# Conv-state transposes between half sums, a second gate product in spare PSUM banks, and the last tile's squares summed in PSUM

## The chip, the cores and the metric

The kernel runs on one core of a Trainium2 chip. The metric is the device time in microseconds of one execution; the median of a few timed runs counts.

## The reference

One layer of a decoder trunk for 512 prompt tokens and 8 sample tokens, in float32. The change touches its last part, cut here to what matters:

```
a, g = split(rmsnorm(h) @ w_up)                  # 1024 -> 2 x 2816
ac = conv_b + causal conv of width 3 over a      # the last rows of a are the new conv state
h = h + (gelu(ac) * g) @ w_down                  # 2816 -> 1024
gate = sigmoid(rmsnorm(h) @ w_ple_gate)          # 1024 -> 1024
h = h + gate * (p @ w_ple)                       # 256 -> 1024
y = rmsnorm(h)                                   # final norm, with the gain g_final
```

Outputs are y for both groups, the recurrent states, and the conv state: 2 rows of 2816 for the prompt, and for each of the 8 samples its old second row and one new row.

## The kernel before

The kernel keeps all activations transposed: channels on partitions, the 520 tokens along the free dimension, split into two halves of 260 that fill the two banks of a PSUM accumulator. Each float32 operand is split into a high and a low part (`whi`/`wlo` for weights, `xah`/`xal`, `xbh`/`xbl`, `ach`/`acl`, `pxh`/`pxl` for activations), and a product is three matmuls (high x high, high x low, low x high) per chunk of 128 rows and token half, six per chunk. `product` (L459) issues them on TensorE (PE). Weights come in units; SP loads `raw`, ScalarE (ACT) copies it to `whi`, VectorE (DVE) subtracts to get `wlo`. Two units are in flight, and ACT and DVE prepare the unit two ahead (`ahead`) when PE has finished one.

Sections run in a fixed order: A, V, B, C, D, E, then F (up-projection and conv, 11 rounds of 4 units), G (down-projection), and H (gates and per-layer input). Each engine follows its own program in order, joined by counting semaphores. There is no planner: the order is written out.

**G.** Each of 8 output tiles of 128 channels needs 22 chunks, in two half sums of 11 chunks (66 matmuls each), so 16 half sums in 4 rounds of 4. After the second half sum of a tile, DVE adds it to `hT` (`residual`), ACT writes `xbh`, DVE writes `xbl`, and GpSimd (POOL) adds the tile's squares to `ssq`.

**H.** For each output tile `j` PE computes a gate product of 8 chunks (48 matmuls) into `acc[0]` and a linear product of 2 chunks (12 matmuls) into `acc[1]`, then `y_tile(j-1)`: one transpose of the sample columns into `ob` and four transposes of 128 tokens into a bank of `lvb`. Within the first gate product PE computes the mean squares (`mean_square(1)`), from which ACT and DVE make `rstd`. DVE forms `tg` = gate product x `rstd` (L1473), ACT its sigmoid `sgg` (L1081), DVE `tp` = linear product x `sgg` (L1477) and `hT` += `tp` (L1479). ACT writes `yT` = `hT` x gain (L1086), `y_copy` brings the transposed tile from `lvb` to `ytok`, and POOL adds the tile's squares. The second gate product waits until `tg` of the first has been read out of `acc[0]`.

**The tail.** After the last product PE transposes the conv state `cs` (22 chunks, 10 columns each) in six groups of up to four into the two `lvb` banks by turns; DVE and ACT copy them to `csr`. Then `y_tile(7)` follows, and the sum of `ssq` over channels (L782) into `mb`: five float32 matmuls, shown as ten instructions. ACT takes the root (L1094), DVE the reciprocal `rt` (L1492), then ACT scales columns 0 to 383 of each row block of `ytok` (L1102) and DVE columns 384 to 1023 (L1500); SP issues the stores of `csr` and then of the five row blocks, the fifth being the samples.

The PSUM tensors are `acc[0]`, `acc[1]` and `lvb` (two banks each), `ob` and `mb` (one each), all eight banks.

Of the kernel before, what the change touches and what calls it, by code (L numbers as in the profile page):

```python
# [13 lines left out]
NS = 8  # L14
# [22 lines left out]
L_C, L_F, L_Y = 8, 24, 28  # L37
# [25 lines left out]
def hybrid_layer(nc, x_prompt, x_sample, state_hgrn, state_ret, state_conv, p_prompt, p_sample,  # L63
# [180 lines left out]
    with ctx:  # L244
# [81 lines left out]
        rt_ready = sem("rt_ready")  # L326
        stored = sem("stored")
# [34 lines left out]
        def _(sp):  # L362
# [56 lines left out]
            with sp.Fori(0, 2) as it:  # L419
                for k in range(4):  # L420
                    load("H", k, it, [wpg_v[:, :, it * 4 + k, :], wpl_v[:, :, it * 4 + k, :]])
            yp = y_prompt[0].rearrange("(i p) n -> p i n", p=128)

            for b in range(2):
                sp.wait_ge(lv_free[b], L_Y // 2 + 7 - b)
            sp.dma_start(conv_prompt[0, 0], csr[0:2, :]).then_inc(stored, 16)
            sp.dma_start(conv_sample[0, :, 1, :], csr[2:10, :]).then_inc(stored, 16)
# [14 lines left out]
        def _(pe):  # L442
# [16 lines left out]
            def product(sec, k, it, slot, tile, chunks, w0, xh, xl, first=True, last=True, tper=4,  # L459
                        wait_unit=True, chunk_wait=None):  # L460
# [4 lines left out]
                if first:  # L465
                    pe.wait_ge(acc_free[tile % 2], tidx(sec, tile, it, tper))
                n = len(chunks)
                for i, c in enumerate(chunks):
# [3 lines left out]
                    for q, (wt, xx) in enumerate(((whi, xh), (whi, xl), (wlo, xh))):  # L472
                        for b in range(2):
                            mm = pe.matmul(acc[tile % 2][:, b, 0:HT], wt[slot][:, w],  # L474
# [238 lines left out]
            def mean_square(n):  # L713
# [3 lines left out]
                for b in range(2):  # L717
                    pe.wait_ge(lv_free[b], L_F // 2 + n)
# [18 lines left out]
            with pe.Fori(0, 4) as it:  # L737
                for k in range(4):
                    if k < 2:
                        pe.wait_ge(ac_lo, FC // (2 - k) + 1)  # L740
                    product("G", k, it, k % 2, k // 2, range(11 * (k % 2), 11 * (k % 2) + 11), 0, ach, acl,
                            first=k % 2 == 0, last=k % 2 == 1, tper=2)
# [15 lines left out]
            for j in range(DC):  # L758
                it, k = j // 4, j % 4
                if j == 0:  # L760
                    def wait_tile(c):
                        if c == 6:
                            mean_square(1)
                        pe.wait_ge(xb_lo, 8 + c + 1)
                product("H", k, it, k % 2, 2 * k, C8, 0, xbh, xbl, tper=8,
                        chunk_wait=wait_tile if j == 0 else None)
                product("H", k, it, k % 2, 2 * k + 1, range(2), 8, pxh, pxl, tper=8, wait_unit=False)
                if j:
                    y_tile(j - 1, j - 1)
            pe.wait_ge(cs_ready, FC)  # L770
            for n in range(6):
                wait_bank(7 + n)
# [948 lines left out]
```

## Time and profile before

| | us |
|---|---|
| median of 3 timed runs | 988.9 (987.56 to 989.34) |
| span of the profiled execution | 985.5 |
| PE busy | 961.0 (98%) |
| DVE busy | 526.4 (53%) |
| ACT busy | 394.5 (40%) |
| POOL busy | 237.7 (24%) |

The profile is of one execution and gives no total time of its own, only the span from its first instruction to its last event. Busy PE time is modelled and includes stretches at the lower clock. L12 is line 12 of the kernel. Matmul instructions overlap: the rows give each group's start and its extent.

### The profile page before, as it was taken

Reading aid. Unit: us, or ns where it says so; the run is one execution under the profiler, and the core shown is the slowest. Engines: PE = TensorE matmul, PEld = TensorE weight load, DVE = VectorE, ACT = ScalarE, POOL = GpSimd, SP = SyncE. Lnnn points to the kernel's source line nnn. Section 1 sums busy time; section 2 is a strip of 40 time slices with the busy share of each in tenths; the row PEclk is TensorE's granted clock in tenths of the full one; section 3 lists DMA queues with packets and bytes.
Section 4 is the critical chain, followed back from the end, with each engine's and each line's share of the span. In section 5 each row is a group of like instructions: output and inputs, shape, how many; then the busy total and the mean of one; then the engine's idle time right before and its main releaser. Section 6 shows DMA issues by size and latency. Waiting matters only on the chain.

```text
span 985.5 us, 20971 instructions
## 1 busy us (share of the span) xinstructions
PE 961.0 (98%) x7866; PEld 928.7 (94%) x7866; DVE 526.4 (53%) x620; ACT 394.5 (40%) x524; POOL 237.7 (24%) x279
## 2 busy tenths in 40 slices
PE   7999999999999999999999999999999999999995
PEld 6999998898989999999999999999999999999994
DVE  5332275664754555456657656655566543435454
ACT  5443345363533544443325444444443321222333
POOL 0006075756501111000362111111111131212331
PEclk9999999999999999999999999999999999999998
DMA  7222422212113332353332332223223333322212
GB/s 233 65 86 86 172 76 65 75 35 71 53 53 108 101 90 85 106 188 110 94 97 76 91 102 85 85 87 104 86 85 105 101 93 106 91 85 80 73 36 92
DMA packets 168052, 91.49 MB, mean 93 GB/s; under 512 B 13584, under 2 KB 166560, under 8 KB 167600
## 3 DMA queue, kind: packets, MB, share of 16 engines
q1 hardware_dynamic: 149698, 80.61, 27.4%
q10 hardware_dynamic: 18320, 10.42, 3.7%
q8 instruction: 22, 0.36, 0.2%
q14 instruction: 12, 0.10, 0.0%
HBM read 83.10 MB, written 8.00 MB: 92 GB/s over the span
## 4 chain that ended last, share of the span: by engine, by line
PE 96%; ACT 1%; DVE 1%; DMA 1%; issue 1%; SPq 0%; ACTq 0%; DVEq 0%
PE acc L474 82%; PE lvb L556 3%; PE ob L605 1%; PE ob L606 1%; PE mb L628 1%; PE lvb L671 1%; DMA xtok<-in_x_prompt 1%; PE mb L683 1%; PE lvb L515 0%; PE mb L593 0%; PE mb L665 0%; PE ob L661 0%; PE ob L660 0%; PE lvb L642 0%; PE lvb L523 0%
## 5 line engine op out<-in xcount | busy, mean ns | idle before, releaser
L803 ACT ACTIVATE whi<-raw 128x1024 fp32r<-128x1024 f32 (+2 forms) x132 | 146.5, 1111 | 356.0 <-PE acc L474 354.9
L1123 DVE TENSOR_TENSOR wlo<-raw,whi 128x1024 fp32r<-128x1024 f32 (+2 forms) x132 | 193.2, 1464 | 178.9 <-ACT whi L803 178.9
L474 PE MATMUL acc<-xah,whi 128*128 128x260 f32 x896 | 188.0, 291 | 0.0
L474 PE MATMUL acc<-xah,wlo 128*128 128x260 f32 x896 | 181.5, 284 | 0.0
L474 PE MATMUL acc<-xal,whi 128*128 128x260 f32 x896 | 180.9, 284 | 0.0
L474 PE MATMUL acc<-xbh,whi 128*128 128x260 f32 x832 | 169.1, 284 | 3.2 <-DVE tg L1473 2.4
L474 PE MATMUL acc<-xbh,wlo 128*128 128x260 f32 x832 | 168.3, 284 | 0.0
L474 PE MATMUL acc<-xbl,whi 128*128 128x260 f32 x832 | 168.1, 284 | 0.0
L474 PEld LDWEIGHTS acc<-xah,whi 128*128 128x128 f32 x896 | 139.2, 190 | 8.9 <-issue 8.2
L474 PEld LDWEIGHTS acc<-xah,wlo 128*128 128x128 f32 x896 | 139.0, 190 | 0.0
L474 PEld LDWEIGHTS acc<-xal,whi 128*128 128x128 f32 x896 | 139.0, 190 | 0.0
L474 PEld LDWEIGHTS acc<-xbh,whi 128*128 128x128 f32 x832 | 128.8, 189 | 3.7 <-issue 3.5
L474 PEld LDWEIGHTS acc<-xbh,wlo 128*128 128x128 f32 x832 | 129.0, 189 | 0.0
L474 PEld LDWEIGHTS acc<-xbl,whi 128*128 128x128 f32 x832 | 128.6, 189 | 0.0
L474 PE MATMUL acc<-ach,whi 128*128 128x260 f32 x352 | 70.9, 283 | 0.0
L474 PE MATMUL acc<-ach,wlo 128*128 128x260 f32 x352 | 70.8, 282 | 0.0
L474 PE MATMUL acc<-acl,whi 128*128 128x260 f32 x352 | 70.6, 282 | 0.0
L1617 POOL TENSOR_TENSOR sqt<-hT 128x520 f32 x24 | 37.4, 1556 | 130.9 <-DVE hT L1379 98.0
L1637 POOL TENSOR_TENSOR gg<-gg,cv 128x520 f32<-128x520 f32 x22 | 28.9, 1314 | 118.0 <-DVE gg L1440 115.2
L474 PEld LDWEIGHTS acc<-acl,whi 128*128 128x128 f32 x352 | 54.3, 188 | 0.0
L474 PEld LDWEIGHTS acc<-ach,whi 128*128 128x128 f32 x352 | 54.2, 188 | 0.0
L474 PEld LDWEIGHTS acc<-ach,wlo 128*128 128x128 f32 x352 | 54.1, 188 | 0.0
(283 smaller groups left out, 1253.7 us busy)
## 6 DMA issues: line engine op xcount, KB each, us to landing
raw<-in_w_in SPq DMA_DIRECT2D x96, 256.0 KB, 3.1
raw<-in_w_up SPq DMA_DIRECT2D x88, 256.0 KB, 3.1
raw<-in_w_down SPq DMA_DIRECT2D x16, 384.0 KB, 3.3
raw<-in_w_down SPq DMA_DIRECT2D x16, 320.0 KB, 3.8
raw<-in_w_out SPq DMA_DIRECT2D x16, 256.0 KB, 2.9
raw<-in_w_ple_gate SPq DMA_DIRECT2D x8, 512.0 KB, 3.7
x_transposed<-xstg SPq DMA_DIRECT2D x1, 2080.0 KB, 7.5
hT<-x_transposed ACTq DMA_DIRECT2D x1, 2080.0 KB, 9.3
```

The source lines that it names most:

```text
L474: mm = pe.matmul(acc[tile % 2][:, b, 0:HT], wt[slot][:, w], xx[:, c, b * HT:(b + 1) * HT], start=first and i == 0 and q == 0, stop=last an ...
L556: mm = pe.matmul(lvb[:, l % 2, c * 128:(c + 1) * 128], lk[l % 4][:, c, :], zq[l % 4][:, c].rearrange("k two t -> k (two t)"), start=True, ...
L605: pe.matmul(out, vst[:, h * 64:(h + 1) * 64], sfull[:, h, :], start=True, stop=False)
L606: mm = pe.matmul(out, head(sst, h), head(lq[3], h), start=False, stop=True)
L628: mm = pe.matmul(mb[64 * h2:64 * h2 + 64, b:b + 1], ss[64 * h2:64 * h2 + 64, b, :], qs8[64 * h2:64 * h2 + 64, b:b + 1], start=True, stop=True)
L671: pe.matmul(level(b), k8[:], vblk[:, 512 * b:512 * b + 512], start=True, stop=True).then_inc(lv_full, 1)
L683: mm = pe.matmul(mb[:, b:b + 1], rsm[:, b, :], qs8[:, b:b + 1], start=True, stop=True)
L803: act.activation(whi[k % 2][:, 0:n], raw[k % 2][:, 0:n], ACT.Copy).then_inc(hi_ready, 1)
L1123: dve.tensor_tensor(wlo[k % 2][:, 0:n], raw[k % 2][:, 0:n], whi[k % 2][:, 0:n].bitcast(fp), SUB).then_inc(lo_ready, 1)
L1617: step(pool.tensor_tensor(sqt[:], hT[:, j, :], hT[:, j, :], MUL))
L1637: pool.tensor_tensor(gg[:], gg[:], cv[:], MUL).then_inc(act_ready, 1)
```

## The change

- On PE the last of G's four rounds is written out. `conv_rows(n)` transposes up to four chunks of the conv state into bank `n % 2` of `lvb`; two such groups follow each of the first three half sums of this round. ACT copies the even groups and DVE the odd ones to `csr`, at the end of their work for that half sum. SP issues the two conv stores between the two rounds of H loads.
- In H the gate product of tile 1 goes into `lvb` and not into `acc[0]`. PE waits for `tg` of this tile before `y_tile(0)` writes `lvb`.
- POOL adds the squares of seven tiles. DVE squares the eighth into `tg`, and PE sums both over channels into the same columns of `mb` (`token_sums`), the older seven first. `y_tile(7)` comes last on PE; DVE scales its columns (896 to 1023) from `lvb`, and the sample columns 512 to 1023 from `ob`, straight from PSUM. ACT computes a root of a constant after its last sigmoid.

```diff
 M_B, M_C, M_F, M_G = 3, 27, 47, 48
-L_C, L_F, L_Y = 8, 24, 28
+L_C, L_F, L_S, L_H, L_Y = 8, 24, 26, 32, 34
 MERGES = LV + 1
...
         rt_ready = sem("rt_ready")
+        sq_last = sem("sq_last")
         stored = sem("stored")
...
                     load("G", k, it, [wdn_v[:, FC // 2 * (k % 2):FC // 2 * (k % 2 + 1), it * 2 + k // 2, :]])
-            with sp.Fori(0, 2) as it:
+            for it in range(2):
                 for k in range(4):
                     load("H", k, it, [wpg_v[:, :, it * 4 + k, :], wpl_v[:, :, it * 4 + k, :]])
+                if it == 0:
+                    for b in range(2):
+                        sp.wait_ge(lv_free[b], L_H // 2)
+                    sp.dma_start(conv_prompt[0, 0], csr[0:2, :]).then_inc(stored, 16)
+                    sp.dma_start(conv_sample[0, :, 1, :], csr[2:10, :]).then_inc(stored, 16)
             yp = y_prompt[0].rearrange("(i p) n -> p i n", p=128)
-            for b in range(2):
-                sp.wait_ge(lv_free[b], L_Y // 2 + 7 - b)
-            sp.dma_start(conv_prompt[0, 0], csr[0:2, :]).then_inc(stored, 16)
-            sp.dma_start(conv_sample[0, :, 1, :], csr[2:10, :]).then_inc(stored, 16)
             for i in range(5):
...
             def product(sec, k, it, slot, tile, chunks, w0, xh, xl, first=True, last=True, tper=4,
-                        wait_unit=True, chunk_wait=None):
+                        wait_unit=True, chunk_wait=None, into=None):
...
                     pe.wait_ge(lo_ready, unit(sec, k, it) + 3)
-                if first:
+                if first and into is None:
                     pe.wait_ge(acc_free[tile % 2], tidx(sec, tile, it, tper))
+                sums = acc[tile % 2] if into is None else into
                 n = len(chunks)
...
                         for b in range(2):
-                            mm = pe.matmul(acc[tile % 2][:, b, 0:HT], wt[slot][:, w],
+                            mm = pe.matmul(sums[:, b, 0:HT], wt[slot][:, w],
                                            xx[:, c, b * HT:(b + 1) * HT],
...
                 for b in range(2):
-                    pe.wait_ge(lv_free[b], L_F // 2 + n)
+                    pe.wait_ge(lv_free[b], (L_F, L_H)[n] // 2)
                     pe.matmul(lvb[:, b, 0:HT], ones1024[:], ssq[:, b * HT:(b + 1) * HT],
...
-            with pe.Fori(0, 4) as it:
-                for k in range(4):
-                    if k < 2:
-                        pe.wait_ge(ac_lo, FC // (2 - k) + 1)
-                    product("G", k, it, k % 2, k // 2, range(11 * (k % 2), 11 * (k % 2) + 11), 0, ach, acl,
-                            first=k % 2 == 0, last=k % 2 == 1, tper=2)
+            def half_sum(k, it):
+                if k < 2:
+                    pe.wait_ge(ac_lo, FC // (2 - k) + 1)
+                product("G", k, it, k % 2, k // 2, range(11 * (k % 2), 11 * (k % 2) + 11), 0, ach, acl,
+                        first=k % 2 == 0, last=k % 2 == 1, tper=2)
+            def conv_rows(n):
+                pe.wait_ge(lv_free[n % 2], L_S // 2 + n // 2)
+                for j in range(4 * n, min(4 * n + 4, FC)):
+                    mm = pe.transpose(lvb[0:10, n % 2, (j % 4) * 128:(j % 4 + 1) * 128], cs[:, j, :], ident)
+                mm.then_inc(lv_full, 1)
+            with pe.Fori(0, 3) as it:
+                for k in range(4):
+                    half_sum(k, it)
+            pe.wait_ge(cs_ready, FC)
+            for k in range(4):
+                half_sum(k, 3)
+                if k < 3:
+                    conv_rows(2 * k)
+                    conv_rows(2 * k + 1)
...
                         pe.wait_ge(xb_lo, 8 + c + 1)
+                if j == 1:
+                    for b in range(2):
+                        pe.wait_ge(lv_free[b], L_Y // 2)
                 product("H", k, it, k % 2, 2 * k, C8, 0, xbh, xbl, tper=8,
-                        chunk_wait=wait_tile if j == 0 else None)
+                        chunk_wait=wait_tile if j == 0 else None, into=lvb if j == 1 else None)
                 product("H", k, it, k % 2, 2 * k + 1, range(2), 8, pxh, pxl, tper=8, wait_unit=False)
+                if j == 1:
+                    pe.wait_ge(acc_free[0], tidx("H", 2, 0, 8) + 1)
                 if j:
                     y_tile(j - 1, j - 1)
-            pe.wait_ge(cs_ready, FC)
-            for n in range(6):
-                wait_bank(7 + n)
-                for j in range(4 * n, min(4 * n + 4, FC)):
-                    mm = pe.transpose(lvb[0:10, (7 + n) % 2, (j % 4) * 128:(j % 4 + 1) * 128], cs[:, j, :], ident)
-                mm.then_inc(lv_full, 1)
-            y_tile(7, 13)
-            pe.wait_ge(ssq_ready, 25)
+            def token_sums(t, last):
+                for i in (0, 4, 1, 2, 3):
+                    n = 128 if i < 4 else NS
+                    mm = pe.matmul(mb[0:n, i:i + 1], t[:, i * 128:i * 128 + n], ones1024[:, 0:1],
+                                   start=not last and i == 0, stop=last and i == 3)
+                return mm
+            pe.wait_ge(ssq_ready, 24)
             wait_misc(M_G, 0, 0, 0)
-            for i in range(5):
-                n = 128 if i < 4 else NS
-                mm = pe.matmul(mb[0:n, i:i + 1], ssq[:, i * 128:i * 128 + n], ones1024[:, 0:1],
-                               start=True, stop=True)
-            mm.then_inc(misc_full, 1)
+            token_sums(ssq, False)
+            pe.wait_ge(sq_last, 1)
+            token_sums(tg, True).then_inc(misc_full, 1)
+            y_tile(7, 7)
...
             def inverse_rms(n):
-                act.wait_ge(lv_full, L_F + 2 * n + 2)
+                act.wait_ge(lv_full, (L_F, L_H)[n] + 2)
                 for b in range(2):
...
                         residual("G", k // 2, it, 2, 24)
+                    if nxt and k < 3:
+                        w = min(512, FF - 2 * k * 512)
+                        act.wait_ge(lv_full, L_S + 2 * k + 1)
+                        act.activation(csr[:, 2 * k * 512:2 * k * 512 + w], lvb[0:10, 0, 0:w],
+                                       ACT.Copy).then_inc(lv_free[0], 1)
...
                 act.activation(sgg[:], tg[:], ACT.Sigmoid).then_inc(sig_ready, 1)
+                if j == DC - 1:
+                    act.activation(ssx[:, 5:6], eps[:], ACT.Sqrt)
                 done("H", 2 * k + 1, it, 8)
...
                     y_copy(j - 1, j - 1)
-            for n in range(1, 6, 2):
-                w = 512 if n < 5 else 256
-                act.wait_ge(lv_full, L_Y + 7 + n + 1)
-                act.activation(csr[:, n * 512:n * 512 + w], lvb[0:10, 0, 0:w], ACT.Copy).then_inc(lv_free[0], 1)
             act.wait_ge(misc_full, M_G + 1)
...
             act.wait_ge(rt_ready, 1)
-            act.wait_ge(lv_free[0], L_Y // 2 + 7)
-            act.wait_ge(lv_free[1], L_Y // 2 + 7)
-            act.wait_ge(ys_taken, 2)
+            act.wait_ge(lv_free[1], L_Y // 2 + 3)
+            act.wait_ge(ys_taken, 1)
             for i in range(5):
...
                 for b in range(2):
-                    dve.wait_ge(lv_free[b], L_F // 2 + n + 1)
+                    dve.wait_ge(lv_free[b], (L_F, L_H)[n] // 2 + 1)
                 step(dve.reciprocal(rstd[:], rstd[:]))
...
                         low()
+                    if nxt and k < 3:
+                        n = 2 * k + 1
+                        w = min(512, FF - n * 512)
+                        dve.wait_ge(lv_full, L_S + n + 1)
+                        dve.tensor_copy(csr[:, n * 512:n * 512 + w], lvb[0:10, 1, 0:w]).then_inc(lv_free[1], 1)
...
                 done("H", 2 * k, it, 8)
-                dve.tensor_tensor(two(tg[:]), ps2(0), two(rstd[:]), MUL).then_inc(acc_free[0], 1)
+                gate = lvb[:, :, 0:HT] if j == 1 else ps2(0)
+                dve.tensor_tensor(two(tg[:]), gate, two(rstd[:]), MUL).then_inc(acc_free[0], 1)
                 done("H", 2 * k + 1, it, 8)
...
                     dve.tensor_copy(ytok[0:NS, 4, 0:512], ob[0:NS, :]).then_inc(ys_taken, 1)
-            for n in range(0, 6, 2):
-                dve.wait_ge(lv_full, L_Y + 7 + n + 1)
-                dve.tensor_copy(csr[:, n * 512:n * 512 + 512], lvb[0:10, 1, :]).then_inc(lv_free[1], 1)
-            y_copy(7, 13)
-            dve.tensor_copy(ytok[0:NS, 4, 512:1024], ob[0:NS, :]).then_inc(ys_taken, 1)
+            dve.wait_ge(h_new, DC + 1)
+            dve.tensor_tensor(tg[:], hT[:, DC - 1, :], hT[:, DC - 1, :], MUL).then_inc(sq_last, 1)
             dve.wait_ge(misc_free, M_G + 1)
...
             dve.wait_ge(rt_ready, 1)
-            dve.wait_ge(lv_free[0], L_Y // 2 + 7)
-            dve.wait_ge(lv_free[1], L_Y // 2 + 7)
-            dve.wait_ge(ys_taken, 2)
+            dve.wait_ge(lv_free[0], L_Y // 2 + 4)
+            dve.wait_ge(lv_full, L_Y + 8)
             for i in range(5):
                 n = 128 if i < 4 else NS
-                dve.tensor_scalar(ytok[0:n, i, YSPLIT:], ytok[0:n, i, YSPLIT:], rt[0:n, i:i + 1], None,
-                                  MUL).then_inc(y_scaled[1], 1)
+                if i < 4:
+                    last, from_sbuf = lvb[:, 1, i * 128:(i + 1) * 128], 896
+                else:
+                    last, from_sbuf = ob[0:NS, :], 512
+                dve.tensor_scalar(ytok[0:n, i, YSPLIT:from_sbuf], ytok[0:n, i, YSPLIT:from_sbuf], rt[0:n, i:i + 1],
+                                  None, MUL)
+                dve.tensor_scalar(ytok[0:n, i, from_sbuf:], last, rt[0:n, i:i + 1], None, MUL).then_inc(y_scaled[1], 1)
...
             step(pool.memset(ssq[:], 0.0))
-            with pool.Fori(0, 2) as it:
-                step.loop(it, 4)
-                for k in range(4):
-                    pool.wait_ge(h_new, it * 4 + (k + 2))
-                    taken()
-                    squares(it * 4 + k, 16)
-            step.end(2)
+            with pool.Fori(0, DC - 1) as it:
+                step.loop(it, 1)
+                pool.wait_ge(h_new, it + 2)
+                taken()
+                squares(it, 16)
+            step.end(DC - 1)
```

## Rows read from the trace of the kernel before

**Rows 1.** The page's shares of the chain that ended last, by engine.

```profile
PE 96%; ACT 1%; DVE 1%; DMA 1%; issue 1%; SPq 0%; ACTq 0%; DVEq 0%
```

**Rows 2.** Waits of PE from 20 us on: total us, times, longest us.

```profile
PE acc L474 <- DVE tg L1473: 2.4, 1, 2.4
PE lvb L774 <- ACT ytok L1074: 1.9, 1, 1.9
PE lvb L556 <- ACT zq L894: 1.1, 1, 1.1
```

**Rows 3.** The chain in order of time from 850 us: start us, us, what.

```profile
849.96 56.65 PE acc L474 x472
906.61 0.51 issue
...
909.22 3.41 DVE rstd L1405
...
913.50 8.96 PE acc L474 x60
...
922.57 0.44 PE lvb L755 x4
923.01 7.21 PE acc L474 x60
```

**Rows 4.** Stretches: us; busy of PE, PEld, DVE, ACT, POOL; granted clock; DMA share; GB/s.

```profile
911.10:913.50 2.40, 0.04 (x1) 0.03 (x1) 2.22 (x2) 0.07 (x1) 0.00 (x0) 1.00 0.00 0
913.50:917.00 3.50, 3.50 (x17) 3.50 (x18) 1.51 (x3) 3.09 (x4) 0.05 (x1) 0.54 0.00 0
...
971.90:974.80 2.90, 2.51 (x19) 1.34 (x19) 1.13 (x2) 1.17 (x2) 1.39 (x2) 1.00 0.00 0
...
251.70:254.80 3.10, 3.10 (x17) 3.10 (x16) 3.07 (x4) 2.98 (x9) 2.18 (x1) 0.50 0.54 161
218.00:222.00 4.00, 4.00 (x37) 4.00 (x36) 3.87 (x5) 2.97 (x8) 3.76 (x6) 1.00 0.14 39
```

**Rows 5.** Tail by time: start us, us, engine, line, operation, count [idle before].

```profile
968.37 0.64 ACT L1081 ACTIVATE sgg<-tg 128x520 f32<-128x520 f32 x1 [4.77 <-DVE tg L1473]
...
969.84 0.70 DVE L1479 TENSOR_TENSOR hT<-hT,tp 128x520 f32<-128x520 f32 x1
...
971.90 1.04 PE L774 MATMUL lvb<-cst,cs 128*10 128x128 f32 x8 [1.93 <-ACT ytok L1074]
...
975.58 1.08 PE L782 MATMUL mb<-ones,ssq 128*128 128x1 f32 x10
...
975.78 0.69 DVE L1468 COPY ytok<-lvb 128x512 f32<-128x512 f32 x1 [0.75 <-PE lvb L755]
...
977.37 2.39 DVE L1500 TENSOR_SCALAR ytok<-ytok,rt 128x640 f32<-128x640 f32 x5
978.01 2.88 SPq L432 DMA_DIRECT2D out<-ytok  x4
```

**Rows 6.** DVE, then ACT, then SP at the gate stage's start, columns as before.

```profile
886.48 0.70 DVE L1379 TENSOR_TENSOR hT<-acc,hT 128x520 f32<-128x520 f32 x1 [4.82 <-PE acc L474]
...
890.08 1.80 DVE L1383 SCALAR_TENSOR_TENSOR xbl<-hT,vc,xbh 128x520 fp32r<-128x520 f32 x1
...
915.45 0.70 DVE L1477 TENSOR_TENSOR tp<-acc,sgg 128x520 f32<-128x520 f32 x1 [2.10 <-ACT sgg L1081]
...
916.80 1.49 DVE L1123 TENSOR_TENSOR wlo<-raw,whi 128x1280 fp32r<-128x1280 f32 x1
...
913.43 1.28 ACT L1081 ACT_TABLE_LOAD   x1 [4.32 <-DVE tg L1473]
914.73 0.64 ACT L1081 ACTIVATE sgg<-tg 128x520 f32<-128x520 f32 x1
...
918.46 0.37 SPq L385 DMA_DIRECT2D raw<-in_w_ple_gate  x1
```

**Rows 7.** GB/s of all transfers from 965 us, in slices of 0.625 us.

```profile
GB/s 26 0 0 0 0 0 0 0 0 0 0 0 0 0 0 0 0 36 108 36 0 0 347 393 406 406 400 406 406 413 229 0 0 0 0 0 0 0 0 0
```

## The prediction

> **What bounds the kernel now.** First the shares of the chain that ended last, by engine [rows 1]: TensorE (PE) carries 96% of it, so a change pays where PE stands still or runs slowly, and in the tail behind its last product. PE's waits name these places [rows 2]: after the first 20 us only one exceeds 2 us, 2.4 us for `tg` before the second gate product; next is 1.9 us for `ytok` in the tail's conv transposes. Then take the chain in order of time [rows 3]. The down-projection runs without a gap at 56.65 / 472 = 0.120 us per matmul; 0.51 us stand before `mean_square(1)`; at 909.22 us the chain leaves PE for the reciprocal of `rstd` (3.41 us) and for `tg`, and the product that follows takes 8.96 us where the later ones take 7.21. The windows tell why [rows 4]: PE stands still from 911.1 to 913.5 us at a granted clock of 1.00, then the clock is 0.54 on average, so nearly always at the lower of its two levels, 1.2 GHz, until 917 us. The tail is a ladder of single steps up to the first output store, issued at 978.01 us [rows 5]. No weight load ends a wait here.
>
> The profile's span is 985.5 us and gives no total of its own; the median of the timed runs is 3.4 us more. I sum against the span and add these 3.4 us unchanged.
>
> **Part 1: the 22 conv transposes go between the half sums.** They leave the tail (that gain is in part 3) and enter a stretch where PE never waits, so they are paid in full. Four `y_tile` transposes of the same 128 columns take 0.44 us between two products [rows 3], 0.11 each: 22 x 0.11 = **+2.4 us**. Eight conv transposes behind a wait took 1.04 us [rows 5], 0.13 each with the latency of the last, which a product behind them covers: 2.9 us is the upper end, 2.2 the lower. Could the copies to `csr` hold PE? The banks alternate, and from the third group on each needs a copy that was asked for one half sum earlier (66 x 0.120 = 7.9 us). The tightest is DVE's behind an odd half sum: before, the residual starts at 886.48 us, a `wlo` follows, and `xbl` ends at 890.08 + 1.80 = 891.9 [rows 6]; a copy of 512 columns took 0.69 [rows 5], so 892.6 us, 6.1 us after the residual's start. PE asks after 7.9: 1.8 us to spare. ACT has less to do. Behind the last odd half sum no copy stands, so `xbl`, the squares and `mean_square(1)` keep their pace, and the 0.51 us stay.
>
> The two conv stores move on SP's queue from behind all H loads to between those of its two rounds. They wait for copies made two half sums before H begins, and the load behind them goes out only at 918.46 us, when a `wlo` frees its buffer [rows 6]. Two issues like that of this load (0.37 us) fit ahead of it: 0. Writing out rounds of the loops on PE and SP removes turns at which PE shows no idle time: 0.
>
> **Part 2: the second gate product goes to `lvb`.** Both banks are free once ACT has read the mean squares, so before DVE's reciprocal starts at 909.22, and the unit's `wlo` precedes that reciprocal on DVE. At 911.1 PE goes straight on. The wait of 2.4 us goes, and with it the cause of the low clock, 8.96 - 7.21 = 1.75 us [rows 3]: **-4.1 us**. What is late next: the linear part of tile 1 needs `acc[1]`, free when `tp` ends at 915.45 + 0.70 = 916.15 us [rows 6]; PE arrives at 911.1 + 48 x 0.120 = 916.9, 0.7 us behind it. PE ends the 60 matmuls at 918.3 and meets the **new wait** before `y_tile(0)`: `tg` of tile 1 must have been read out of `lvb`. On DVE that `tg` stands behind a `wlo` that ends at 916.80 + 1.49 = 918.3 [rows 6]; with 0.70 of its own, like `tp`, it ends at 919.0. PE waits 0.7 us, and behind it wait `y_tile(0)` and all of tile 2. The third product starts at 919.0 + 5 x 0.11 = 919.6 us instead of 923.01: net **-3.4 us**. Bounds: -4.1 if `tg` slipped ahead of `wlo`, -1.6 if the low clock stays. From there a tile takes 7.21 + 0.55 = 7.76 us as before; `whi` and `wlo` keep their distance, since DVE and ACT follow PE.
>
> Does a wait of 0.7 us lower the clock? The trace has one of 1.1 us [rows 2], before 200 us, and no low clock after it. The clock fell behind the 2.4 us of standing, and twice within the recurrence, behind 32 one-column matmuls of `mb` at L628 (251.7 to 254.8 us is one of the falls [rows 4]; two further such places have none). I take no fall.
>
> **Part 3: the tail.** Times are on the axis of before. `hT` 7 ends at 969.84 + 0.70 = 970.5 us; DVE squares it, by the same row 0.70: 971.3; PE sums the squares into `mb`, ten instructions in 1.08 us [rows 5] and 0.1 for the first weight load: 972.5. The ten that sum the older seven tiles run while PE waits: `hT` 6 was ready a whole tile, 7.8 us, before `hT` 7. ACT's two roots and DVE's two reciprocals took from the last sum's end, 975.58 + 1.08 = 976.66, to the first scaling at 977.37 [rows 5] 0.7 us: 973.2. `y_tile(7)` runs beside them, by the eight transposes in 1.04 us some 0.8 us for five: 973.3. What it needs, `yT` 7, and `y_copy` 6 are over before 971.90, where PE's wait for `ytok` ended [rows 5].
>
> DVE now scales each row block in two pieces, 512 columns from SBUF and 128 from PSUM. No row has such a piece. Nearest: five `tensor_scalar`s, four of them with 640 columns, in 2.39 us, 0.48 each; a copy of 512 columns from PSUM, 0.69 [rows 5]. The ends are 0.48 for both pieces and 0.48 + 0.69 = 1.17; since the second piece has a quarter of that copy's columns I take 0.75, nearer the first. The first store goes out at 973.3 + 0.75 + 0.03 = 974.1 instead of 978.01: **-3.9 us**, ends -4.2 and -3.5. The later blocks are paced by the transfers, which run at about 400 GB/s from 978.75 to about 984 us [rows 7]: 512 KB take 1.3 us, longer than 0.75 or 1.17. So the end follows the first store.
>
> The switch from sigmoid to root is asked for ahead, by a dummy root after the last sigmoid: 968.37 + 0.64 = 969.0 [rows 5], + 1.28 for the load [rows 6] and 0.24 for the root, guessed like ACT's small ones, = 970.5, when `yT` 7 may start. Hidden, 0 to 0.1. The Trainium skill, "ScalarE: Activation LUTs", section "What ACT_TABLE_LOAD costs", charges a switch with the load and a drain of about 1.38 us more. By that figure `yT` 7 would start 1.3 us late and the first scaling some 0.6 us late; the sum would be -4.3. The trace disagrees: the load of 913.43 ends at 914.71 and `sgg` starts at 914.73 [rows 6].
>
> **Sum:** +2.4 - 3.4 - 3.9 = **-4.9 us**: span 980.6, time 988.9 - 4.9 = **984.0 us**.
>
> **The rivals.**
> A. The 1.75 us of the clock are not earned: the low clock comes anyway (0.5 us of standing at 906.6, 0.7 at 918.3), or the median run of before did not have it. For: the three runs lie 1.8 us apart, the size of one fall, and like places in the recurrence brought it two times in four. Against: the profiled run has it behind its longest stop. 984.0 + 1.75 = 985.8.
> B. The tail gives back about 1 us: after its last product PE does one-column sums and transposes, so it may drop to the low clock for the last sums and `y_tile(7)` (1.2 + 0.8 us, at most twice as long), or the first scaling takes 1.17. Against: from 971.9 to 974.8 us the clock was 1.00 [rows 4]. 985.0.
> C. The stores end no earlier: their own traffic and last landing bound the end. Then +2.4 - 3.4 remain: 987.9. Against: between 977.5 and 978.75 us nothing is transferred [rows 7].
> D. **Slower.** The conv transposes bring the low clock into the densest stretch: each of the three insertions (0.9, 0.9, 0.7 us) and the new wait are followed by a fall of 1.75 us. Three falls give 989.3, no change; four give 984.0 + 7.0 = 991.0, slower: it decides from the fourth. For: light work on PE has preceded falls. Against: `y_tile` puts 0.55 us of transposes between products six times before the last tile with no fall, and from 218 to 222 us, with 16 narrow matmuls for score blocks, the clock is 1.00 [rows 4]. The Trainium skill, "TensorE: Matmul & The Clock Gate", section "Part 4: PE-mode transpose", says that transposes do not count as busy for the clock; that would be this rival, and the `y_tile` places do not bear it out at their length.
> E. A new wait in place of the old: a copy or `tg` reaches PE later than derived. Each microsecond costs one; above 2.9 us it is no change, 987 or more.
>
> **Numbers.** My sum 0.60 (its own range 982.8 to 985.2), A 0.20, B 0.11, C and E together 0.05, D 0.04 (0.03 of it with the fourth fall). A change counts as faster or slower only beyond 0.2% (2 us), about what this measurement can tell. Faster: 0.60 + 0.20 + 0.11 = 0.91; same: 0.05 + 0.01 = 0.06; slower 0.03. The range takes in A, the 0.9 us by which single runs stray and the upper prices: 982.0 to 986.7.
>
> **What would show it.** Part 1: 22 transposes in three places between the last half sums, no idle time of PE there, granted clock 1.00, the down-projection 2.4 us longer. Part 2: no stop at the second gate product, 7.2 us for it, and a wait of about 0.7 us for `tg` before the first `ob` transpose. Part 3: from `hT` 7 (970.5 before) to the first store 3.6 us instead of 7.5, stores still at 400 GB/s. I am wrong if the clock falls inside the down-projection, if the new wait is well over 1 us, or if the stores start earlier but end no earlier.

## The result and the profile after

The changed kernel takes **984.2 us** (median of 4 runs, 982.7 to 984.4) against 989.1 (987.6 to 989.5): ratio 0.995, interval 0.9938 to 0.9962. 984.0 was predicted. A second set of 5 runs gave 984.2 again, ratio 0.9955 (0.9941 to 0.9969). The profiled execution has a span of 982.5 us.

PE's waits from 20 us on, to be read beside [rows 2]: total us, times, longest us.

```profile
PE lvb L559 <- ACT zq L918: 1.1, 1, 1.1
PE mb L799 <- DVE tg L1519: 0.8, 1, 0.8
PE acc L477 <- issue: 0.8, 1, 0.8
PE acc L477 <- DVE arl L1380: 0.6, 1, 0.6
PE ob L771 <- DVE tg L1505: 0.6, 1, 0.6
PE lvb L722 <- issue: 0.5, 1, 0.5
```

The 2.4 us for `tg` and the 1.9 us for `ytok` are gone. New are 0.6 us for `tg` before `y_tile(0)` and 0.8 us in which the tail waits for the last tile's squares.

The same columns as [rows 4], for the changed kernel:

```profile
296.00:299.40 3.40, 3.40 (x18) 3.40 (x18) 1.67 (x5) 0.93 (x2) 2.46 (x3) 0.50 0.68 195
880.00:906.30 26.30, 26.30 (x223) 25.83 (x223) 9.32 (x8) 6.08 (x7) 3.53 (x2) 1.00 0.26 77
911.40:923.90 12.50, 11.89 (x95) 11.55 (x96) 7.93 (x7) 5.33 (x8) 1.88 (x3) 1.00 0.21 63
...
972.20:975.20 3.00, 1.83 (x15) 1.55 (x15) 1.21 (x5) 1.93 (x6) 0.00 (x0) 1.00 0.00 0
```

The clock is 1.00 in the down-projection and in the first gate products, where [rows 4] had the fall. But this execution has a fall at 296 us, far ahead of any edit, which the profiled execution of before has not (clock 1.00 there). So its absolute times stand 1.8 us late up to the last half sums, and the spans differ by 3.0 us where the change moved 4.8.

The conv transposes between the half sums, on PE, in order of time:

```profile
880.18 1.04 PE L750 MATMUL lvb<-cst,cs 128*10 128x128 f32 x8
880.97 0.49 PE L477 MATMUL acc<-ach,whi 128*128 128x260 f32 x2
...
888.99 1.03 PE L750 MATMUL lvb<-cst,cs 128*10 128x128 f32 x8
...
897.77 0.82 PE L750 MATMUL lvb<-cst,cs 128*10 128x128 f32 x6
```

Eight transposes start at 880.18 and the product resumes at 880.97. DVE at the start of the gate stage answers to [rows 6]:

```profile
894.51 0.67 DVE L1489 COPY csr<-lvb 10x512 f32<-10x512 f32 x1
...
906.56 0.70 DVE L1405 TENSOR_TENSOR hT<-acc,hT 128x520 f32<-128x520 f32 x1 [5.03 <-PE acc L477]
...
913.46 3.40 DVE L1431 RECIPROCAL rstd<-rstd 128x520 f32<-128x520 f32 x1 [1.64 <-ACT rstd L1049]
...
919.69 0.70 DVE L1509 TENSOR_TENSOR tp<-acc,sgg 128x520 f32<-128x520 f32 x1 [2.10 <-ACT sgg L1110]
...
921.04 1.49 DVE L1149 TENSOR_TENSOR wlo<-raw,whi 128x1280 fp32r<-128x1280 f32 x1
922.45 0.69 DVE L1505 TENSOR_TENSOR tg<-lvb,rstd 128x520 f32<-128x520 f32 x1
```

The copy of `csr` stands behind `xbl` and ends at 895.2 us, 2.6 us before PE's next transposes at 897.77. `tg` from `lvb` follows `wlo` and ends at 923.1. The last residual of the down-projection, here at 906.56, stands in before at 902.32:

```profile
902.32 0.70 DVE L1379 TENSOR_TENSOR hT<-acc,hT 128x520 f32<-128x520 f32 x1 [5.06 <-PE acc L474]
```

By the chain, as in [rows 3], the third product follows:

```profile
923.90 7.21 PE acc L477 x60
```

The tail answers to [rows 5]:

```profile
969.93 1.28 ACT L1112 ACT_TABLE_LOAD   x1
...
970.73 0.70 DVE L1511 TENSOR_TENSOR hT<-hT,tp 128x520 f32<-128x520 f32 x1
...
971.46 0.70 DVE L1519 TENSOR_TENSOR tg<-hT 128x520 f32<-128x520 f32 x1
...
972.22 1.27 PE L799 MATMUL mb<-ones,tg 128*128 128x1 f32 x10 [0.79 <-DVE tg L1519]
...
973.46 0.60 PE L774 MATMUL lvb<-cst,yT 128*128 128x128 f32 x4
973.52 0.26 ACT L1121 ACTIVATE rt<-mb,eps 128x4 f32<-128x4 f32 x1 [0.79 <-PE mb L799]
...
974.21 0.48 DVE L1532 TENSOR_SCALAR ytok<-ytok,rt 128x512 f32<-128x512 f32 x1
974.61 0.34 DVE L1534 TENSOR_SCALAR ytok<-lvb,rt 128x128 f32<-128x128 f32 x1
...
975.02 2.89 SPq L434 DMA_DIRECT2D out<-ytok  x4
```

From the end of `hT` 7 (the residual stream's last tile, 971.43) to the first output store 3.59 us pass; before, it was 978.01 - 970.54 = 7.47. From the first store to the end it is 982.48 - 975.02 = 7.46 us, before 985.46 - 978.01 = 7.45: the end follows the first store. The rates of all transfers, as in [rows 7], are the same, one step of 3.1 us earlier:

```profile
GB/s 0 0 0 0 0 0 0 0 0 0 0 0 0 0 0 0 0 256 406 387 406 406 406 400 419 315 7 0 0 0 0 0 0 0 0 0 0 0 0 0
```

### The profile page after: what moved, and what is told of

Its sections match the earlier page's. It is cut to its first block and busy times, and to the rows that moved or that the text cites. A ratio compares the mean times of both kernels' runs of the same rounds, so it can differ in the third digit from the quotient of the medians.

```text
span 982.5 us, 20952 instructions
## 1 busy us (share of the span) xinstructions
PE 961.6 (98%) x7876; PEld 930.2 (95%) x7876; DVE 526.7 (54%) x624; ACT 394.6 (40%) x525; POOL 235.6 (24%) x277
## 5 line engine op out<-in xcount | busy, mean ns | idle before, releaser
L477 PE MATMUL acc<-xbh,whi 128*128 128x260 f32 x816 | 165.3, 284 | 0.8 <-issue 0.8
L477 PE MATMUL acc<-xbh,wlo 128*128 128x260 f32 x816 | 164.4, 283 | 0.0
L477 PE MATMUL acc<-xbl,whi 128*128 128x260 f32 x816 | 164.2, 283 | 0.0
L477 PEld LDWEIGHTS acc<-xbh,whi 128*128 128x128 f32 x816 | 125.8, 188 | 1.1 <-issue 1.0
L477 PEld LDWEIGHTS acc<-xbh,wlo 128*128 128x128 f32 x816 | 125.8, 188 | 0.0
L477 PEld LDWEIGHTS acc<-xbl,whi 128*128 128x128 f32 x816 | 125.5, 188 | 0.0
```

The costliest lines, as they stand in the source:

```text
L477: mm = pe.matmul(sums[:, b, 0:HT], wt[slot][:, w], xx[:, c, b * HT:(b + 1) * HT], start=first and i == 0 and q == 0, stop=last and i == n ...
```

## The experiments

Each kernel was timed beside the kernel before on its chip. The sign of an edit stands against the kernel named with it; edits are cut to their main lines.

| kernel | median us | ratio to before (interval) | expected us |
|---|---|---|---|
| undo_gate | 987.4 | 0.9984 (0.9975-0.9992) | 987.6 |
| gate_only | 985.4 | 0.9962 (0.9949-0.9976) | 985.7 |
| conv_only | 988.9 | 0.9996 (0.9987-1.0006) | 989.5 |
| conv_twice | 986.9 | 0.9979 (0.9968-0.9990) | 986.6 |
| filled_stop | 987.6 | 0.9991 (0.9982-1.0000) | from 987.0 |
| wlo_early | 983.8 | 0.9947 (0.9935-0.9960) | 983.4 |
| no_root | 984.5 | 0.9958 (0.9944-0.9971) | 984.7 |
| conv_idle | 984.2 | 0.9953 (0.9940-0.9966) | 982.1 |
| both | 982.9 | 0.9937 (0.9924-0.9950) | 981.3 |
| both_act | 983.0 | 0.9944 (0.9930-0.9958) | 981.1-981.3 |
| mixed | 982.6 | 0.9937 (0.9924-0.9951) | 982.1 |
| changed_again | 984.2 | 0.9955 (0.9941-0.9969) | 984.2 |

**undo_gate**, on the changed kernel:

```diff
-                        chunk_wait=wait_tile if j == 0 else None, into=lvb if j == 1 else None)
+                        chunk_wait=wait_tile if j == 0 else None)
```

> The changed kernel with the second gate product back in acc[0]. Theory (the stop of 2.4 us for tg and the low clock that it causes are what part 2 saved, 4.1 us, less a new wait of 0.6 to 0.7): 3.4 us slower than the changed kernel's 984.2, so 987.6; the trace shows the stop of 2.4 us and a product of about 9 us behind it. Rival (the low clock there is not caused by the stop): the product behind it keeps 7.2 us and the loss is 1.6 us, 985.8.

The median is the theory's, but the profiled run does not bear out the theory's reason: it shows the stop and no fall behind it, and a fall in the tail instead:

```profile
914.90:917.40 2.50, 0.18 (x2) 0.00 (x0) 2.39 (x2) 0.00 (x0) 0.00 (x0) 1.00 0.00 0
917.50:921.00 3.50, 3.50 (x29) 3.50 (x30) 1.53 (x3) 3.10 (x4) 0.08 (x1) 1.00 0.02 5
972.90:976.70 3.80, 2.98 (x16) 2.45 (x15) 1.01 (x4) 2.09 (x6) 0.00 (x0) 0.69 0.00 0
```

```profile
917.48 7.44 PE acc L477 x60
...
925.47 7.21 PE acc L477 x60
```

The product behind the stop took 7.44 us, 0.23 more than a later one. The tail's last sums and `y_tile(7)` ran slowly:

```profile
973.78 1.81 PE L793 MATMUL mb<-ones,tg 128*128 128x1 f32 x10 [0.80 <-DVE tg L1513]
...
975.62 1.06 PE L774 MATMUL lvb<-cst,yT 128*128 128x128 f32 x4
```

1.81 us instead of 1.27, 1.06 instead of 0.60, and from `hT` 7 (972.99) to the first store (977.65) 4.66 us instead of 3.59. So in this execution the loss is the stop (1.8 us, worked out below) and 1.1 us in the tail. The 3.2 us of the median do not show that the stop causes the fall.

**gate_only** puts the second gate product into the spare banks, alone, on the kernel before:

```diff
-                        chunk_wait=wait_tile if j == 0 else None)
+                        chunk_wait=wait_tile if j == 0 else None, into=lvb if j == 1 else None)
...
+                gate = lvb[:, :, 0:HT] if j == 1 else ps2(0)
-                dve.tensor_tensor(two(tg[:]), ps2(0), two(rstd[:]), MUL).then_inc(acc_free[0], 1)
+                dve.tensor_tensor(two(tg[:]), gate, two(rstd[:]), MUL).then_inc(acc_free[0], 1)
```

> The kernel before with the second gate product in lvb and nothing else changed. Theory: 3.4 us faster than before, 989.1 - 3.4 = 985.7, with no low clock at the start of the gate stage, a wait of 0.6 us before y_tile(0) and a tail as before. Rival (the parts are not independent, the low clock comes at another place of the gate stage): 1.6 us faster, 987.5.

3.6 us faster than its chip's 989.0, where the theory says 3.4; the interval, 2.4 to 5.0 us, leaves the rival's 1.6 out. The profiled run has the tail of before (967.65 to 975.13 us, 7.48) and a wait of 0.6 us before `y_tile(0)`.

**filled_stop**, on the kernel before:

```diff
+                if j == 1:
+                    pe.wait_ge(hi_ready, unit("H", k, it) + 1)
+                    for _ in range(18):
+                        pe.matmul(ob[:, 0:HT], whi[1][:, 0:128], xbh[:, 0, 0:HT], start=True, stop=True)
```

> The kernel before with 18 extra matmuls of the product's shape, whose result nobody uses, issued by PE in the 2.4 us in which it waits for tg; 18 x 0.120 = 2.2 us fit in. Theory (standing still brings the low clock behind it): no low clock behind the wait, the second product takes 7.2 instead of 8.96 us, 1.75 us faster in every run in which the kernel before has this fall, so up to 1.75 below its median. Rival (the fall has another cause, such as the mean-square stretch before it): the product still takes about 9 us and the time is that of before.

```profile
912.90:915.40 2.50, 2.37 (x20) 2.16 (x18) 2.41 (x2) 0.00 (x0) 0.00 (x0) 1.00 0.00 0
915.50:919.00 3.50, 3.50 (x29) 3.50 (x30) 1.51 (x3) 3.09 (x4) 0.05 (x1) 1.00 0.02 5
```

No fall in the profiled run; the product took 7.45 us. The median is 1.1 us below before's 988.7, and the interval reaches 1.0000, so the size is only roughly known. As undo_gate shows, an unfilled stop has no fall in some runs, so this profile can't prove the cause.

The traces do part the stop from the fall. From the start of DVE's reciprocal of `rstd` to the start of the third product:

| profiled execution | us | what lies between |
|---|---|---|
| before, conv_only | 13.79, 13.76 | stop and fall |
| undo_gate, filled_stop | 12.28, 12.28 | stop (unfilled, filled), no fall |
| after, gate_only | 10.44, 10.44 | neither; the new wait |
| wlo_early | 9.67 | neither, no wait |

So the edit saves 1.84 us where no fall stood behind the stop and 3.35 where one did; the fall alone is 1.51. gate_only's 3.6 us leave 1.7 to the clock, filled_stop's 1.1 would be all the clock's; the intervals (2.4 to 5.0 us and 0 to 1.8) don't fix the share of runs that have the fall.

What it comes with is shown in part. Of the profiled executions with an unfilled stop, before and conv_only have no fall near 296 us and one behind the stop; undo_gate has one near 296 us and none behind the stop. The profiled execution of gate_only, without a stop, has neither. That speaks for the stop as a cause, but filled_stop too has a fall near 296 us (0.54 from 295.0 to 298.4 us), so it can't tell what filling did. The cause of the fall behind the stop stays open.

**conv_twice**, on the changed kernel:

```diff
+                for _ in range(2):
-                for j in range(4 * n, min(4 * n + 4, FC)):
+                    for j in range(4 * n, min(4 * n + 4, FC)):
```

> The changed kernel with each of the 22 conv transposes issued twice, so that the insertions between the half sums are 1.7, 1.7 and 1.3 us long. Theory (PE is the bound there, each transpose costs 0.11 us and the clock stays): 2.4 us slower than 984.2, 986.6, granted clock 1.00 throughout the down-projection. Rival (transposes bring the low clock): one to three falls of 1.75 us each in the down-projection, 988.4 to 991.9.

2.7 us slower than 984.2. In the trace the three insertions take 1.66, 1.67 and 1.23 us instead of 0.79, 0.79 and 0.58, together 2.4 more, and their stretch keeps its clock:

```profile
880.00:906.00 26.00, 26.00 (x223) 25.06 (x222) 9.31 (x8) 6.08 (x7) 3.53 (x2) 1.00 0.25 72
```

One fall would give 988.4. The rival is refuted for insertions up to 1.7 us.

**conv_only** moves the conv state alone; the tail keeps POOL's eighth square, and its order is `y_tile(7)`, then the sums.

On the changed kernel without its gate edit:

```diff
-            pe.wait_ge(ssq_ready, 24)
-            token_sums(ssq, False)
-            pe.wait_ge(sq_last, 1)
-            token_sums(tg, True).then_inc(misc_full, 1)
             y_tile(7, 7)
+            pe.wait_ge(ssq_ready, 25)
+            for i in range(5):
+                mm = pe.matmul(mb[0:n, i:i + 1], ssq[:, i * 128:i * 128 + n], ones1024[:, 0:1], start=True, stop=True)
```

> The kernel before with only the conv transposes, their copies and the two conv stores moved; the last tile's squares stay on POOL, y_tile(7) comes before the sums and the scaling reads SBUF. Theory (the tail is then set by POOL: hT 7 ends at 970.5, two POOL instructions end at 973.5, sums 1.2, roots and reciprocals 0.7, first piece 0.6, first store 976.0 instead of 978.0): the tail gains 2.0, the down-projection costs 2.4, so 0.4 us slower than before, 989.5. Rival (the conv transposes were the whole length of the tail): the tail gains 3.9 and the kernel is 1.5 us faster than before, 987.6.

```profile
974.44 0.70 DVE L1500 TENSOR_TENSOR hT<-hT,tp 128x520 f32<-128x520 f32 x1
...
975.56 1.05 POOL L1635 TENSOR_TENSOR sqt<-hT 128x520 f32 x1 [5.20 <-DVE hT L1500]
...
976.79 1.28 POOL L1636 TENSOR_TENSOR ssq<-ssq,sqt 128x520 f32<-128x520 f32 x1 [0.18 <-POOL sqt L1635]
...
978.13 1.99 PE L796 MATMUL mb<-ones,ssq 128*128 128x1 f32 x10 [1.40 <-POOL ssq L1636]
...
981.48 2.89 SPq L434 DMA_DIRECT2D out<-ytok  x4
```

POOL is the tail's bound, as expected: its second instruction ends at 978.07, and the sums follow at once. They ran at the low clock here (1.99 us), which adds 0.8 to the expected 5.5 us from `hT` 7 to the first store (6.34, before 7.47). The time is that of before within its interval: **part 1 alone gains nothing**; the theory's loss of 0.4 us and a zero can't be told apart, the rival's 1.5 us gain can be ruled out.

**no_root**, on the changed kernel:

```diff
-                if j == DC - 1:
-                    act.activation(ssx[:, 5:6], eps[:], ACT.Sqrt)
```

> The changed kernel without the root of a constant after the last sigmoid. Theory (a switch costs the load of 1.28 us and no more): the load starts behind y_copy 6 on ACT, at 972.74 by the changed kernel's trace, ends at 974.03, and the roots start 0.5 us later than 973.52: 984.7. Rival (a drain of 1.38 us comes on top, as the Trainium skill has it under 'ScalarE: Activation LUTs', 'What ACT_TABLE_LOAD costs'): the roots start 1.9 us later, 986.1.

```profile
970.19 0.70 DVE L1509 TENSOR_TENSOR hT<-hT,tp 128x520 f32<-128x520 f32 x1
...
972.21 1.28 ACT L1119 ACT_TABLE_LOAD   x1
...
973.50 0.26 ACT L1119 ACTIVATE rt<-mb,eps 128x4 f32<-128x4 f32 x1
...
975.00 2.89 SPq L434 DMA_DIRECT2D out<-ytok  x4
```

The load runs behind `y_copy` 6 (which ends at 972.19), and the root follows 0.01 us behind it. From `hT` 7 (970.89) to the first store it is 4.11 us, 0.52 more than 3.59. The median's 0.3 us are within the spread. The charge for a drain that the Trainium skill has ("ScalarE: Activation LUTs", "What ACT_TABLE_LOAD costs") does not appear.

**wlo_early** lets ACT and DVE prepare the unit two ahead before `sgg` and `tp` in the first tile (the call `ahead("H", k, it)` goes up, for `j == 0`; DVE's part is shown).

```diff
+                if j == 0:
+                    ahead("H", k, it)
                 dve.wait_ge(sig_ready, 12 + j + 1)
...
-                if j < DC - 2:
+                if 0 < j < DC - 2:
                     ahead("H", k, it)
```

> The changed kernel; for the first tile of the gate stage ACT makes whi and DVE makes wlo of the unit two ahead before sgg and tp, in time in which both only wait. Theory (the new wait of 0.6 us before y_tile(0) comes from tg of tile 1 queued behind that wlo on DVE): the wait is gone, y_tile(0) runs without a restart, the third product starts 0.8 us earlier relative to the second, 983.4. Rival (DVE is late for another reason, the mean-square chain): the wait stays, 984.2.

```profile
918.46 1.48 DVE L1152 TENSOR_TENSOR wlo<-raw,whi 128x1280 fp32r<-128x1280 f32 x1
...
922.12 0.70 DVE L1508 TENSOR_TENSOR tg<-lvb,rstd 128x520 f32<-128x520 f32 x1 [0.84 <-PE lvb L477]
```

DVE is now free when the second gate product ends, `tg` follows it directly, and PE has no wait there; the third product starts 0.77 us earlier (9.67 us instead of 10.44 in the table above). Its profiled run has the low clock in the last sums (from `hT` 7 to the first store 4.72 us), and the median gives 0.4 of the 0.8 us, with an interval that holds both.

**conv_idle**, on the changed kernel, shortened:

```diff
                         if c == 6:
+                            conv_rows(0)
                             mean_square(1)
...
             token_sums(ssq, False)
+            conv_rows(1)
+            conv_rows(2)
             pe.wait_ge(sq_last, 1)
             token_sums(tg, True).then_inc(misc_full, 1)
             y_tile(7, 7)
+            conv_rows(3)
+            conv_rows(4)
+            conv_rows(5)
```

> The changed kernel with the conv transposes taken out of the down-projection again and put where PE waits anyway: one group before mean_square(1), two between the sums over the older tiles and those over the last, three behind y_tile(7); they go into ob, acc and lvb banks, the last copies come behind the scaling and the two conv stores behind the output stores. Theory (part 1 costs 2.4 us only because PE has no idle time in the down-projection): 2.4 us are saved and about 0.3 us come back, the transfer of 110 KB behind the output stores: 982.1. Rival (the late conv stores, not the output stores, end the kernel, some 2 us later): 984.1, no gain.

The first store goes out 3.59 us after `hT` 7, as in the changed kernel, so the two groups in PE's wait for the last squares are free. The group before `mean_square(1)` is not: from DVE's last residual to the reciprocal of `rstd` it is 7.61 us instead of 6.90. ACT copies that group to `csr` (909.19 to 909.78 us) ahead of its table load, which in the changed kernel ran under ACT's wait for the mean squares and now starts at 909.80, so `rstd` is 0.71 late. Of the 2.4 us 1.7 are saved. And the end comes 982.82 - 973.61 = 9.21 us later instead of 7.46. SP's first output stores and its last conv store, and the rates:

```profile
973.61 2.89 SPq L431 DMA_DIRECT2D out<-ytok  x4
...
978.84 0.49 SPq L436 DMA_DIRECT2D out<-csr  x1
```

```profile
GB/s 0 0 0 0 0 0 0 0 0 0 0 0 0 0 0 360 419 380 406 406 406 400 413 234 126 36 0 0 0 0 0 0 0 0 0 0 0 0 0 0
```

The output transfers end at about 980; 126 and 36 GB/s are the conv stores behind them, slow for their 110 KB. The rival holds: the late conv stores end the kernel. By these rows, -2.41 + 0.71 + 1.75 = 0.05, and the median is the changed kernel's.

**both** joins conv_idle and wlo_early; **both_act** also lets ACT issue the conv stores.

```diff
-            sp.dma_start(conv_prompt[0, 0], csr[0:2, :]).then_inc(stored, 16)
-            sp.dma_start(conv_sample[0, :, 1, :], csr[2:10, :]).then_inc(stored, 16)
+            act.dma_start(conv_prompt[0, 0], csr[0:2, :]).then_inc(stored, 16)
+            act.dma_start(conv_sample[0, :, 1, :], csr[2:10, :]).then_inc(stored, 16)
```

> The edits of wlo_early and conv_idle together on the changed kernel. Theory (they are independent): 0.8 + 2.1 = 2.9 us below 984.2, 981.3. Rival (the end is held by the late conv stores): 983.4.

> The edits of both, and the two conv stores issued by ACT behind its last copy, not by SP behind the output stores. Theory (in both the first output store went out at 971.50 us but the span ended at 980.7, 9.2 us later instead of 7.5, because the conv stores were issued last): the output stores end the kernel again, 1.6 to 1.8 us below both's 982.9, 981.1 to 981.3. Rival (the conv stores' transfer itself holds the output stores up): 982.9.

both is 1.3 us faster than the changed kernel, with 9.21 us behind the first store again. Here the 0.71 us do not count, since PE no longer waits for `tg`. In both_act the stores ran beside the output stores:

```profile
GB/s 0 0 0 0 0 0 0 0 0 190 393 413 413 393 393 413 419 344 141 44 7 25 0 0 0 0 0 0 0 0 0 0 0 0 0 0 0 0 0 0
```

The end came 979.93 - 970.12 = 9.81 us after the first output store: no gain, my theory of the issue order fails, and the rival's cause (the conv transfer itself, when late) stands.

**mixed**, on `both`: three groups go back between the half sums, the other three stay in PE's waits, and SP stores the conv state ahead of the output:

```diff
                 half_sum(k, 3)
+                if k < 3:
+                    conv_rows(3 + k)
...
-            conv_rows(3)
-            conv_rows(4)
-            conv_rows(5)
...
+            sp.wait_ge(csa, 3)
+            sp.wait_ge(csd, 3)
+            sp.dma_start(conv_prompt[0, 0], csr[0:2, :]).then_inc(stored, 16)
+            sp.dma_start(conv_sample[0, :, 1, :], csr[2:10, :]).then_inc(stored, 16)
```

> The edits of both, but 10 of the 22 conv transposes back between the last half sums (one group behind each of the first three), one group before mean_square(1) and two in the tail's wait for the last squares, and the conv stores ahead of the output stores. Theory (late conv stores held the end of both and both_act; a transpose costs 0.11 us in the down-projection and nothing in PE's waits): 12 x 0.11 = 1.3 us and the 0.8 us of wlo_early below the changed kernel's 984.2, so 982.1, and from the first output store to the end 7.5 us again. Rival (the two conv stores, issued some 1.5 us ahead of the output stores, now slow these): 982.9 or more.

```profile
971.26 0.29 SPq L430 DMA_DIRECT2D out<-csr  x1
...
972.86 2.91 SPq L436 DMA_DIRECT2D out<-ytok  x4
```

From the first output store to the end it is 980.82 - 972.86 = 7.96 us: nearly the 7.46, with 0.5 us lost to conv stores issued only 1.6 us ahead, so the rival holds in part. 982.6 is the lowest median, 1.6 us below the changed kernel's; against both the intervals can't part them.

**changed_again** is the changed kernel once more, without an edit:

> The changed kernel as it is, for more runs on the same chip as the two others. Expected: 984.2, runs in two groups about 1.5 us apart by the number of falls to the low clock, the same spread as the kernel before.

984.2 as expected, but the runs, 983.3 to 985.0, form no two clean groups.

## Why the prediction was right

- **Part 1, +2.4.** Before the gate stage DVE's last residual of the down-projection began at 906.56, in before at 902.32: 4.24 us later, of which 1.83 stand already at 872.59 (against 870.76), ahead of the first insertion. The fall at 296 us, 3.4 us at half the clock, accounts for 1.7 of them. Left are 2.41 us. conv_twice confirms the price (2.7), and no fall followed the insertions. The copies had 2.6 us to spare, not 1.8, since PE came later by its own transposes.
- **Part 2, -3.4.** By the chains, the third product starts at 923.90 instead of 923.01, 0.89 later on an axis that is 4.24 late: -3.35. The new wait is 0.61 us, not 0.7, because DVE starts `tg` 0.1 us before `wlo` ends; `y_tile(0)` takes 0.71 instead of 0.55 behind a wait, which gives it back. wlo_early shows that the queue on DVE is the cause. The 1.75 us for the clock were too much for the clock alone: a product behind the stop takes 7.44 us without a fall, so 1.52 are the fall's and 0.23 the stop's. And they were counted in full, though undo_gate's profiled execution has the stop and no fall. Against a run of before without that fall this part is worth 1.84 us. Rival A may therefore hold in a share of the runs; how large a share is open.
- **Part 3, -3.9.** `hT` 7 to the first store: 3.6 us were predicted, 3.59 measured. The terms: square 0.70, sums 1.27 instead of 1.18, roots and reciprocals 0.7, first scaling 0.48 then 0.34, overlapped to 0.74 (0.75 taken). conv_only shows how it divides: with the conv state gone but POOL's square kept the first store came 6.34 us after `hT` 7, or some 5.5 without the 0.8 of the low clock, so by this estimate 2.0 of the 3.9 us are the conv state's.
- **Sum.** Spans: 982.48 - 985.46 = -2.98, with the 1.83 us taken off: -4.8 against -4.9. The medians say -4.9, with an interval from -3.8 to -6.1. That they meet the prediction to 0.1 us is partly luck, since the clock's share of part 2 is not fixed better than to some tenths of a microsecond. What the traces do fix came out near the derived terms: 2.41 us for 2.4, 3.88 for 3.9, and for the stop with its new wait 1.84 where my terms give 3.4 - 1.75 = 1.65.
- **What was wrong:** the 3.4 us between span and time. The changed kernel's profiled run took 984.27 us for a span of 982.5, so 1.8 lie around a span. The rest was that before's profiled execution (mean granted clock 0.990) is one of the quicker ones: in 61 runs of before, those of 0.990 took 987.3 to 988.6 us, those of 0.986 took 990.1 to 990.9. The predicted span of 980.6 was too low as well (982.5), by the fall at 296 us. Neither touches the difference of the medians.
- **Rivals.** B does occur, though not in the first profile: undo_gate, wlo_early and conv_only had the low clock in the last sums, at 1.1, 1.1 and 0.8 us; the two profiled executions of the changed kernel (3.59 and 3.60 us from `hT` 7 to the first store) did not. C did not hold for the changed kernel, because part 1 also takes the conv stores out of the tail; conv_idle shows what it would have cost. I had priced that move at 0; it is worth 1.8 us against stores issued last, and 0.5 us against stores 1.6 us ahead of the output (mixed). D is refuted at these lengths. The Trainium skill, "TensorE: Matmul & The Clock Gate", "Part 4: PE-mode transpose", says that transposes do not count as busy for the clock. These runs do not decide that: PE's wait of 1.1 us for `zq` had no fall behind it either [rows 2].

## What to carry to other kernels

Price a moved step at both ends: in a stretch where the bound engine never waits it costs its full time, and where it left, only what the next bound lets go (conv_only: +2.4 and some -2.0, no gain in sum) until the next edits use the room. When a tail shortens, look at which store is issued last and how fast it can run, not only at the bulk: 110 KB held the end 1.8 us behind 2.1 MB. Before crediting a fall of the clock to a wait, compare several executions by their mean granted clock; one profile holds one draw.

## What the runs showed of the hardware

- The conv stores, 22 and 88 KB from 2 and 8 partitions, move at 126 GB/s or less on their own, where the output stores of 128 partitions reach 400.
- Falls of the granted clock far from any edit differ between executions: the one at 296.0 us in the changed kernel's is missing in before's (clock 1.00 there). A lower mean granted clock goes with a longer run: 0.990 with 987.3 to 988.6 us, 0.986 with 990.1 to 990.9, in the kernel before.
- A stop of PE of 2.4 us was followed by a fall in two of three profiled executions (before, conv_only) and by none in the third (undo_gate). PE's waits of 0.6 us (`tg` of tile 1) and 1.1 us (`zq`), and up to 1.7 us of transposes between products, had none.
- A product of 60 matmuls behind a stop took 7.44 us at full clock, 7.21 without a stop and 8.96 with a fall.
- One-column sums and transposes at the end of PE's work ran at either clock: ten sums 1.27 us, or 1.81 to 1.99.
- In conv_idle a copy of 0.59 us on ACT, ahead of a table load of 1.28 us that had run under a wait, made `rstd` 0.71 us late.
